# Row-half pairing of the 64x64 products in the state-space stage of a two-stack transformer kernel

## The reference, cut to what matters

```python
def step(state, inp):
    r_t, w_t, k_t, v_t, a_t, b_t = inp
    sa = jnp.einsum('bhij,bhj->bhi', state, a_t)
    state = (state * w_t[:, :, None, :]
             + sa[..., None] * b_t[:, :, None, :]
             + v_t[..., None] * k_t[:, :, None, :])
    y_t = jnp.einsum('bhij,bhj->bhi', state, r_t)
    return state, y_t
```

## Time and profile before

| | |
|---|---|
| Median of 3 runs | 3479.65 us |
| The profiled execution | 3479.74 us |
| Its span | 3478.0 us |
| PE busy, share of the span | 3328.0 us, 96% |
| DVE, ACT, POOL busy | 1747.1, 1274.5, 336.6 us |
| First stretch of the changed phase | 536.7 to 637.8 us of the span |
| Second stretch | 1608.3 to 1709.5 us |

### The profile page before, as it was taken

The page is one execution under the profiler, slowest core; times in us unless marked ns, Lnnn a source line. Parts: engine busy times, 40 slices in busy tenths (PEclk is TensorE's granted clock), DMA queues, the critical chain, the costliest instruction groups (busy, mean ns, idle before and its releaser), DMA issues. The chain is left out here.

```text
span 3478.0 us, 52375 instructions
## 1 busy us (share of the span) xinstructions
PE 3328.0 (96%) x21106; PEld 2732.5 (79%) x21106; DVE 1747.1 (50%) x2634; ACT 1274.5 (37%) x1871; POOL 336.6 (10%) x277
## 2 busy tenths in 40 slices
PE   7999999799999999999889999988999998899998
PEld 5888879588888888878778888876888875578886
DVE  4443365564444444355464443556665354666642
ACT  3222356642223222345652222434222232542221
POOL 0000325400000000042500000010000002400000
PEclk9999999899999999999989999999999998999999
DMA  3233320032332223220022232312333240022232
GB/s 113 96 98 106 107 73 4 16 99 97 96 104 89 97 96 107 96 93 25 15 67 97 96 101 93 128 55 79 96 96 105 101 178 4 13 85 97 96 102 80
DMA packets 73607, 295.75 MB, mean 85 GB/s; under 512 B 8160, under 2 KB 9056, under 8 KB 72288
## 3 DMA queue, kind: packets, MB, share of 16 engines
q1 hardware_dynamic: 73440, 293.32, 25.5%
HBM read 291.19 MB, written 2.10 MB: 84 GB/s over the span
## 5 line engine op out<-in xcount | busy, mean ns | idle before, releaser
L441 PE MATMUL bank<-src_hi,tile_hi 128*128 128x512 f32 x2736 | 1078.9, 394 | 26.5 <-DVE tile_lo L522 25.7
L443 PE MATMUL bank<-src_hi,tile_lo 128*128 128x512 f32 x2736 | 1065.7, 389 | 0.0
L442 PE MATMUL bank<-src_lo,tile_hi 128*128 128x512 f32 x2736 | 1065.3, 389 | 0.0
L522 DVE TENSOR_TENSOR tile_lo<-raw_tiles,tile_hi 128x1024 fp32r<-128x1024 f32 (+1 forms) x486 | 625.8, 1311 | 84.7 <-ACT tile_hi L471 68.2
L441 PEld LDWEIGHTS bank<-src_hi,tile_hi 128*128 128x128 f32 x2736 | 514.1, 188 | 146.5 <-DVE tile_lo L522 26.1
L442 PEld LDWEIGHTS bank<-src_lo,tile_hi 128*128 128x128 f32 x2736 | 514.3, 188 | 112.1 <-issue 6.7
L443 PEld LDWEIGHTS bank<-src_hi,tile_lo 128*128 128x128 f32 x2736 | 514.0, 188 | 107.6
L471 ACT ACTIVATE tile_hi<-raw_tiles 128x1024 fp32r<-128x1024 f32 (+1 forms) x486 | 526.6, 1112 | 77.5 <-DMA raw_tiles<-in_b_in 33.2
L441 PE MATMUL bank<-hid_hi,tile_hi 128*128 128x512 f32 x1312 | 514.3, 392 | 25.4 <-DVE tile_lo L522 25.4
L442 PE MATMUL bank<-hid_lo,tile_hi 128*128 128x512 f32 x1312 | 513.2, 391 | 0.0
L443 PE MATMUL bank<-hid_hi,tile_lo 128*128 128x512 f32 x1312 | 512.8, 391 | 0.0
(11 more groups left out here) (338 smaller groups left out, 3168.7 us busy)
## 6 DMA issues: line engine op xcount, KB each, us to landing
raw_tiles<-in_gu SPq DMA_DIRECT2D x264, 512.0 KB, 3.5
raw_tiles<-in_down SPq DMA_DIRECT2D x96, 704.0 KB, 4.1
raw_tiles<-in_w_in SPq DMA_DIRECT2D x46, 512.0 KB, 3.5
raw_tiles<-in_a_in SPq DMA_DIRECT2D x17, 512.0 KB, 3.5
raw_tiles<-in_w_out SPq DMA_DIRECT2D x16, 512.0 KB, 3.6
raw_tiles<-in_w_mem SPq DMA_DIRECT2D x16, 512.0 KB, 3.5
masks<-in_masks SPq DMA_DIRECT2D x4, 1948.0 KB, 8.3
raw_tiles<-in_b_in SPq DMA_DIRECT2D x9, 512.0 KB, 3.6
```

Of the source, the lines that this page charges most:

```text
L441: nc.tensor.matmul(bank, wh, hi[:, kk, 0:p.n], start=(kk == 0), stop=False)
L442: nc.tensor.matmul(bank, wh, lo[:, kk, 0:p.n], start=False, stop=False)
L443: mm = nc.tensor.matmul(bank, wl, hi[:, kk, 0:p.n], start=False, stop=last and (p.kind == "gated" or s == p.h - 1))
L522: v.tensor_tensor(self.tile_lo[:, t, 0:kc * P], self.tile_raw[:, t, 0:kc * P], self.tile_hi[:, t, 0:kc * P].bitcast(F32), ALU.subtract).th ...
```

## The change

The products are sorted into 22 stages. A stage has one or two products of the same pair: a "straight" one, whose result lands in the row half of its operands, and a "crossed" one, whose result lands in the other row half (`rows[r ^ cross]`). In each chunk the upper rows of both are issued, then the lower rows of both products of the stage before. Eleven stages have two products, eleven have one. As a crossed product moves a head to the other half, the other operands are arranged so that each later product meets its partner in the same half. All eight PSUM banks form one ring (in the order 5, 4, 2, 3, 7, 0, 1, 6) over all names but n2, y2 and y3, which add to the banks of n1 and y1. The order of the products on PE, of the keeps on ACT and of the operations on DVE is new, and so is the number of convolution terms after each keep. The sum of terms is still 62.

```diff
+    RWKV_STAGES = (("lt", "v"), ("l", "ka"), ("a", "rk"), ("g", "sq2"), (None, "sq2t"), ("mv", "sq4"), (None, "up1"), ("b", "sq4t"), (None, "up2"),
+                   (None, "sq8"), (None, "up3"), ("c1", None), ("turn", "k"), ("up4t", "up4"), ("c2", None), ("up5", None), (None, "u"), ("q", "w"),
+                   ("mt", "n1"), ("n2", "y1"), ("y2", None), (None, "y3"))
+    RWKV_VECTOR = ("lt", "l", "o32", "o64", "started", "ka", "rk", "g", "up1", "up2", "up3", "up4", "up4t", "up5", "q", "mt")
+    RWKV_SCALAR = ("v", "a", "sq2", "sq2t", "mv", "sq4", "b", "sq4t", "sq8", "c1", "turn", "k", "c2", "u", "w", "n2")
...
-        bank_of = {at: banks[i % 5] for i, at in enumerate(ring)}
+        ring = [banks[i] for i in (5, 4, 2, 3, 7, 0, 1, 6)]
+        bank_of = {at: ring[i % 8] for i, at in enumerate(order)}
         for cc in range(RW):
-            for name in ("l", "n1", "n2", "y1", "y2", "y3"):
-                bank_of[name, cc] = banks[5 + cc]
-        scan_banks = [banks[(len(ring) + e) % 5] for e in range(2)]
+            bank_of["n2", cc] = bank_of["n1", cc]
+            bank_of["y2", cc] = bank_of["y3", cc] = bank_of["y1", cc]
+        scan_banks = [bank_of["mt", 1], bank_of["mt", 2]]
...
+                def rows_of(work, r, c):
+                    (name, cc), lhs, rhs, cross, skip = work
+                    to = rhs[rows[r], :] if rhs.shape[1] == CH else chunk(rhs, c)[rows[r], :]
+                    return nc.tensor.matmul(chunk(bank_of[name, cc], c)[rows[r ^ cross], :], chunk(lhs, c)[rows[r], :], to,
+                                            start=c == 0 and name not in ("n2", "y2", "y3"), stop=(c == NCH - 1), skip_group_check=True)
+
+                def stage(cc, cross=None, straight=None, skip=0):
...
+                    works = [((w[0], cc), w[1], w[2], crossed, skip) for w, crossed in ((cross, 1), (straight, 0)) if w is not None]
+                    for at, _, _, _, _ in works:
+                        if at in order and order.index(at) >= 8:
+                            name, n = order[order.index(at) - 8]
+                            if name in self.RWKV_SCALAR:
+                                pe.wait_ge(kept_a, in_a(name, n))
+                            else:
+                                pe.wait_ge(kept_v, in_v("o64" if name == "l" else name, n))
+                    last = {}
                     for c in range(NCH):
...
+                        for r, some in ((0, works), (1, behind)):
+                            for work in some:
+                                if c >= work[4]:
+                                    last[work[0]] = rows_of(work, r, c)
+                    for work in behind:
+                        last[work[0]].then_inc(multiplied, 1)
+                    behind = works
...
+                    stage(cc, cross=("lt", Fb[cc], Fa[cc]), straight=("v", Fv[cc], ident))
+                    stage(cc, cross=("l", Fa[cc], Fb[cc]), straight=("ka", Fk[cc], Fa[cc]))
+                    stage(cc, cross=("a", Fa[cc], ident), straight=("rk", Fk[cc], Fr[cc]))
...
+                    pe.wait_ge(kept_a, in_a("sq2t", cc))
+                    pe.wait_ge(kept_v, in_v("ka", cc))
+                    stage(cc, cross=("mv", KA[cc], V[cc]), straight=("sq4", L2T[cc], L2[cc]))
...
+                    pe.wait_ge(ends_scaled, cc + 1)
+                    stage(cc, cross=("b", Fb[cc], ident), straight=("sq4t", L2[cc], L2T[cc]))
...
+                pe.wait_ge(multiplied, made("y1", 0))
+                stage(0, cross=("y2", L2T[0], G[0]))
                 for c in range(1, NCH - 1):
                     for e in range(2):
                         step(e, c)
-                    if c <= 2:
-                        product("y1", c, V[c], RK[c])
-                    elif c <= 5:
-                        product("y2", c - 3, L2T[c - 3], G[c - 3])
+                    if c < RW:
+                        pe.wait_ge(multiplied, made("y1", c))
+                        stage(c, cross=("y2", L2T[c], G[c]))
...
-                    more = dict(sq2t=6, mv=4, sq8=8, b=6, c2=6, w=6, n2=8).get(name, 2)
+                    more = dict(sq2=2, sq4=2, b=6, sq8=6, c1=2, u=2, n2=8).get(name, 4)
...
                 masked("lt", LT, "m16T")
                 masked("l", L, "m16")
+                masked("l", O32, "m32")
+                masked("l", O64, "m64")
                 for cc in range(RW):
                     dve.wait_ge(kept_v, in_v("lt", cc))
                     v.tensor_tensor(chunks(IT[cc]), chunks(LT[cc]), mask("ident2"), ALU.add).then_inc(kept_v, 1)
-                masked("l", O32, "m32")
-                masked("l", O64, "m64")
                 masked("ka", KA, "strictT")
+                masked("rk", RK, "inclT")
+                masked("g", G, "inclT")
+                for cc in range(RW):
+                    v.tensor_tensor(chunks(Fb[cc]), chunks(Fb[cc]), end(cc), ALU.mult).then_inc(ends_scaled, 1)
                 increased("up1", IT, IT, "started")
                 for cc in range(RW):
                     v.tensor_tensor(chunks(MT[cc]), mask("ident2"), end(cc), ALU.mult).then_inc(ends_scaled, 1)
+                for cc in range(RW):
+                    v.tensor_tensor(chunks(Fk[cc]), chunks(Fk[cc]), end(cc), ALU.mult).then_inc(ends_scaled, 1)
```

More of the change, by code:

```diff
@@ L1115, in _ @@
             def _(pe):
[L1116 to L1124, removed]
-                    nonlocal behind
[L1127 to L1133, removed]
-                    for c in range(NCH):
[L1135 to L1148, removed]
+                behind = ()
+                def rows_of(work, r, c):
[3 more added lines that the diff above has]
+                                            start=c == 0 and name not in ("n2", "y2", "y3"), stop=(c == NCH - 1), skip_group_check=True)
@@ L1189, in _ @@
                     pe.wait_ge(kept_v, in_v("up1", cc))
-                    product("up2", cc, L[cc], IT[cc])
+                    stage(cc, straight=("up2", L[cc], IT[cc]))
                 for cc in range(RW):
                     pe.wait_ge(kept_a, in_a("sq4t", cc))
-                    product("sq8", cc, LT[cc], L[cc])
-                for cc in range(RW):
-                    product("g", cc, Fb[cc], Fr[cc])
+                    stage(cc, straight=("sq8", LT[cc], L[cc]))
                 for cc in range(RW):
@@ L1198, in _ @@
                     pe.wait_ge(kept_v, in_v("up2", cc))
-                    product("up3", cc, L2[cc], IT[cc])
-                for cc in range(RW):
-                    product("rk", cc, Fk[cc], Fr[cc])
+                    stage(cc, straight=("up3", L2[cc], IT[cc]))
                 for cc in range(RW):
                     pe.wait_ge(kept_v, in_v("up3", cc))
-                    product("turn", cc, IT[cc], ident)
+                    stage(cc, cross=("c1", O32[cc], IT[cc]))
                 for cc in range(RW):
-                    product("c1", cc, O32[cc], IT[cc])
+                    pe.wait_ge(ends_scaled, 2 * RW + cc + 1)
@@ L1207, in _ @@
+                    stage(cc, cross=("turn", IT[cc], ident), straight=("k", Fk[cc], ident))
                 for cc in range(RW):
-                    pe.wait_ge(ends_scaled, RW + 2 * cc + 1)
-                    product("b", cc, Fb[cc], ident)
-                for cc in range(RW):
-                    pe.wait_ge(kept_a, in_a("c1", cc))
-                    product("up4", cc, L[cc], L2T[cc])
-                for cc in range(RW):
-                    product("up4t", cc, L2T[cc], L[cc])
-                for cc in range(RW):
-                    pe.wait_ge(ends_scaled, RW + 2 * cc + 2)
-                    product("k", cc, Fk[cc], ident)
+                    pe.wait_ge(kept_a, in_a("turn", cc))
@@ L1218, in _ @@
+                    stage(cc, cross=("up4t", L2T[cc], L[cc]), straight=("up4", L[cc], L2T[cc]))
                 for cc in range(RW):
                     pe.wait_ge(kept_v, in_v("up4t", cc))
-                    product("c2", cc, O64[cc], IT[cc])
+                    stage(cc, cross=("c2", O64[cc], IT[cc]))
                 for cc in range(RW):
                     pe.wait_ge(kept_a, in_a("c2", cc))
-                    product("up5", cc, LT[cc], L2[cc])
-                for cc in range(RW):
-                    product("n1", cc, K[cc], V[cc])
+                    stage(cc, cross=("up5", LT[cc], L2[cc]))
@@ L1252, in _ @@
                 for cc in range(RW):
-                    product("y3", cc, states_behind(cc), Fr[cc], skip=1)
-                finish()
+                    pe.wait_ge(multiplied, made("y2", cc))
+                    stage(cc, straight=("y3", states_behind(cc), Fr[cc]), skip=1)
+                stage(RW)
                 for cc in range(RW):
```

70 lines of the change are left out of this document (28 added, 42 removed).

## The result

The changed kernel takes 3511.55 us (median of four runs, 3509.91 to 3513.27), the kernel before 3479.23 beside it. The ratio is 1.0099, 95% interval 1.0087 to 1.0111: 32 us slower. The forecast was 3477, 2 us faster, with 3491 as its upper end.

The account below looks back on a forecast made before the run. PE was taken to bound the kernel, busy 96% of the span. Of 30.9 us won a stretch 24 go into waits, leaving 6.4; the clock returns 5.3: -1.2 a stretch, -2.3 for two, 3479.7 to 3477, range 3465 to 3491.

Parts of the forecast that it names:

- The pace of the array: PE's paired stages: four 64x64 tiles run at once, 64 records in 0.936 us, 0.0146 us each.
- gated-attention burst: 64 records of 32x64 tiles in 1.21 us, 0.0149 us apart, read as both column halves working at once.
- price of 0.936 us for a paired stage: PE's stage of two products costs 0.936 us, making the stream 61.8 us instead of 92.7 per stretch.
- supply check: Instruction queue: a packet takes 1.04 us, paired stages want one per 1.9 us, so it was said to fit.
- rival B: In paired stages four tiles run, but slower than 0.0146 us a record; +5.1 us a stretch at 1.05; chance 0.18.
- rival C: Column halves of a row group take turns, a paired stage takes 1.87 us; +25 us a stretch, 3530; chance 0.07.
- the same layout: All four engines' lists of a stretch laid out in time: 102.0 us before, 95.6 after, 6.4 less.
- The waits: PE's waits for other engines in each stretch on the new list, together 24.7 us.
- ka's bank: PE waits 7.1 us, about 6.6 us into the stretch, because DVE keeps ka only after 15 operations.
- The clock: PE gaps of 3 us or more tend to bring spells of up to 6.8 us at 1.2 GHz; four such gaps.
- part 3: Clock step for each stretch: eight layouts with slow spells average 100.9 us, giving back 5.3 of 6.4 us.
- The sign: Whole kernel slightly faster: pairing wins 30.9 us a stretch on PE's stream, net -1.2 us a stretch.

Follow-up runs that it names:

- e9: Changed kernel with ka kept first, products issued one after the other, 60 of 62 convolution terms and their sums left out: 3487.33 us, ratio 1.0028.
- e10: Changed kernel with ka kept first, still paired, 60 of 62 convolution terms and their sums left out: 3490.79 us, ratio 1.0037.
- e6: Changed kernel without 60 of the 62 convolution terms on ACT and their 60 sums on POOL: 3495.21 us, ratio 1.0052.
- e2: Changed kernel with DVE keeping ka right after l, ahead of the other two masks of l: 3503.64 us, ratio 1.0071.
- e3: Changed kernel with the two products of a stage issued one after the other: 3503.49 us, ratio 1.0069.
- e1: Changed kernel plus four wait-free streams of 768 PE records after the first load: two tiles took 24.7 us, four tiles from a loop 13.9 us.
- e8: Changed kernel plus four more wait-free streams (128 columns, 96 columns, two-tile loop, three-packet loop body): two-tile loop took 22.4 us for 762 records.
- e5: Kernel before with one more always-met wait instruction ahead of each 64x64 call of the stage: 3723.09 us, ratio 1.0701.

## Why the prediction was wrong, point by point

**The pace of the array** was right: four starts together, 0.0147 a record in bursts (1.88 us for 128), as taken from the gated-attention burst. The forecast's price of 0.936 us for a paired stage is the array's price, and the array was not what a paired stage waited for.

**The failed step** is this price of 0.936 us in the sum, and behind it the supply check inside rival B, which let it stand. The check read the transfer time of a packet (1.04 us) from the earlier trace rows, compared it with the demand (a packet per 1.9 us) and said "That fits". A transfer is only the middle part of a cycle in which one packet follows the other: 1.1 us until the transfer begins, 1.0 to 1.4 for it, 1.35 to 1.5 until PE goes on, 3.46 to 4.0 together. The row for that was there: 25 packets in 101.1 us is one per 4.0 us, and no row showed a quicker sequence. In the whole trace of the kernel before no two of the 130 packets start less than 3.3 us apart. The burst of 64 records, on which the price of 0.936 rested, was half a packet, so it could not show the supply, as the prediction said and then gave little weight. Rival B was thus the right place with the wrong price: not 0.98 or 1.05 a paired stage but a floor of 128 records per 3.5 to 4 us, that is 1.73 to 2.0 us for a paired stage of 64 records, nearly the 1.87 of rival C. This also says how the kernel before stood: 128 records per 3.74 us, just at the floor, so there was little for pairing to win in straight code; e9 and e10 show none.

**The layout with the floor.** These are estimates of mine, worked out afterwards; no trace has them. With one rule added to the same layout (128 records become available no sooner than 3.74 us after PE began on the 128 before), the list of before stays at 102.0 us and the new one goes from 95.6 to 113.3; with 3.46 it is 109.3, with 3.9 it is 115.8 (and before would be 104.7). Without the terms it gives 106.5 (measured 106.4 and 110.3), with ka first as well 104.7 (106.9 and 107.6). What is left between 113.3 and the measured 117.3 is of the size of the clock's part, but no run split it off.

**The waits** were right in place, and the large ones in size: 6.9 us for ka's bank against 7.1; the long waits for ACT were 3.5 and 3.65, where I had 3.4 (sq8) and 3.9 (k's bank). Ahead of b PE waited 1.75 us where I had 3.0, ahead of up3 0.7 where I had 1.6, and the 2.0 ahead of mv did not appear; packet gaps stand ahead of each and made PE come later. In sum PE waited 9.5 us for ACT's keeps in four pieces, 7.8 of it under ACT's name in the view. The long gap began 10.0 us into the stretch and not 6.6, behind two packet gaps of 0.8 and 1.9.

**The clock** fell at the three long waits as forecast, in spells of 3.4 and 6.8 us, and twice more behind issue gaps of 2.1 us and less, which part 3 did not have. Its price was smaller than in part 3 where stages are paired: from 553.95 on, at a granted clock of 0.50, 129 records took 3.45 us, about the time of a packet. By this estimate the slower array was mostly covered by the supply; no run takes the clock apart from the rest.

**The sign.** Pairing was to take 30.9 us off PE's stream. PE's busy time fell by 15.5 us in the first stretch (by 18.2 between e9 and e10, which have the terms left out and ka first), and 15.3 us of packet gaps took that back; what is missing to 30.9 no run splits up. The new order then cost its waits, 16.4 us in the first stretch with the one ahead of b, and some clock. Of the 16 us a stretch about 8 go away with the convolution terms ahead of keeps (e6), 3 to 4 with ka's late keep (e2) and 3 to 4 with the pairing (e3), each undone alone; they overlap (e10 has the first two out and is 9 to 10 us a stretch better) and are no sum.

No version beat the kernel before. What remains untried: products that share the same stationary operand (ka with rk, lt with g, u with w, q with mt) as one call of 128 columns would need fewer instructions, which is what the floor asks for; it needs another layout of the banks. Nor did any run try the stage from a loop over chunks.

## What to carry to other kernels

Before making TensorE issue faster, divide: how many us does a packet of instructions last now, and how many after the change? In straight code at one f32 record per weight load the floor was 128 records per 3.5 to 4 us in these traces; small tiles reach it at two at a time, and beyond it concurrency in the array is worth nothing, unless the code is a loop or each instruction does more work. In a profile the sign is idle time of PE that ends in "issue" every 128 records (an issue gap off that count can be a wait that the view does not name, as the 1.75 us ahead of b); and a new order that lets PE stand for 3.5 to 6.9 us at a time, as here, also pays for the half clock that followed each of these gaps.

## What the runs showed that was not expected

- Instructions came to PE at a packet of 256 per 3.46 us in the probe's steady part (e1), and at one per 3.3 to 4.6 us between the waits of e10, although the transfer takes about 1 us; a loop whose body is three packets is not fetched again (e8).
- A met wait that stands as an instruction of its own cost PE 0.079 us (e5).
- In e1 the two-tile stream with 32 columns took 39.8 us for 768 records at a granted clock of 0.51, although PE was busy in 39.80 of 39.80 us; the same two tiles with 64 columns were at 1.00. Busy time as the profile counts it does not say whether the clock stays.
